# Zero-padding a 24-row product to 128 rows in a decoder-step kernel

## What is computed

```
S_new = exp(b_last)[..., None] * S + einsum('bshk,bshv->bhkv', kc, vc)   # s has one token
```

## Time and profile before

| what | value |
|---|---|
| timed runs, median | 1084.79 us |
| profiled execution, its own time | 1083.09 us |
| its span, first to last instruction | 1081.3 us |
| mean granted PE clock | 0.993 |
| PE busy | 1049.4 us (97%), 8530 matmuls |
| DVE busy | 570.6 us (53%) |
| ACT busy | 430.4 us (40%) |
| POOL busy | 1.4 us, 6 instructions |

### The profile page before, as it was taken

One profiled execution on the slowest core, in us unless ns is written; L12 is line 12 of the kernel. 1 busy time (PEld: TensorE's weight loads), 2 busy tenths in 40 slices (PEclk: granted clock), 3 DMA queues, 4 the chain that ended last, 5 costly groups with the idle time before them and its releaser, 6 DMA issues.

```text
span 1081.3 us, 21621 instructions
## 1 busy us (share of the span) xinstructions
PE 1049.4 (97%) x8530; PEld 1031.0 (95%) x8530; DVE 570.6 (53%) x1026; ACT 430.4 (40%) x586; POOL 1.4 (0%) x6
## 2 busy tenths in 40 slices
PE   6999999999999999999999997899999999999997
PEld 6999999999998899999999997799999999999997
DVE  5756655765665988633333333755545445422223
ACT  6443542444344888522222234732232332322222
POOL 0000000000000000000000000000000000000000
PEclk9999999999999999999999999999999999999999
DMA  7322232232222332333323343033233233133322
GB/s 216 98 81 78 80 99 73 85 99 80 80 88 67 89 87 83 94 87 97 94 82 95 97 158 98 20 98 90 85 97 96 78 97 92 55 92 96 95 78 79
DMA packets 182567, 98.23 MB, mean 91 GB/s; under 512 B 3784, under 2 KB 181192, under 8 KB 182408
## 3 DMA queue, kind: packets, MB, share of 16 engines
q1 hardware_dynamic: 164376, 88.62, 27.9%
q10 hardware_dynamic: 18080, 9.04, 2.8%
q0 software_dynamic: 80, 0.15, 0.0%
HBM read 90.79 MB, written 7.00 MB: 90 GB/s over the span
## 4 chain that ended last, share of the span: by engine, by line
PE 92%; DVE 3%; ACT 2%; DMA 1%; issue 1%; SPq 0%; DVEq 0%; ACTq 0%
PE proj L1178 79%; PE pr L1264 5%; DMA tmp<-in_x_prompt 1%; PE pi L1313 1%; PE pr L1318 1%; PE pr L1381 1%; PE pr L1287 1%; PE pi L1295 1%; PE pi L1381 1%; PE pi L1301 0%; ACT wh L320 0%; PE proj L1328 0%; DVE tmp L1077 0%; DVE acts L1065 0%; DVE raw L1157 0%
## 5 line engine op out<-in xcount | busy, mean ns | idle before, releaser
L1178 PE MATMUL proj<-acts,wh 128*128 128x260 f32 x4864 | 796.9, 286 | 11.1 <-DVE acts L1065 9.3
L1178 PEld LDWEIGHTS proj<-acts,wh 128*128 128x128 f32 x4864 | 668.7, 189 | 18.0 <-DVE acts L1065 10.9
L1178 PE MATMUL proj<-acts,wl 128*128 128x260 f32 x2432 | 490.7, 283 | 0.0
L1178 PEld LDWEIGHTS proj<-acts,wl 128*128 128x128 f32 x2432 | 375.5, 189 | 0.0
L681 DVE TENSOR_TENSOR wl<-raw,wh 128x1024 fp32r<-128x1024 f32 (+2 forms) x164 | 190.9, 1164 | 273.4 <-ACT wh L320 273.3
L320 ACT ACTIVATE wh<-raw 128x1024 fp32r<-128x1024 f32 (+2 forms) x164 | 165.8, 1011 | 355.7 <-PE proj L1178 352.5
L1264 PE MATMUL pr<-tmp 128*128 128x64 f32 (+1 forms) x512 | 65.8, 271 | 0.1
L1264 PEld LDWEIGHTS pr<-tmp 128*128 128x128 f32 x512 | 62.5, 191 | 0.9 <-DVE tmp L908 0.3
L766 DVE TENSOR_TENSOR tmp<-tmp 128x256 f32<-128x256 f32 x56 | 23.7, 423 | 24.4 <-PE pr L1264 24.3
L637 ACT ACTIVATE acts<-tmp 128x520 f32 (+1 forms) x21 | 13.5, 641 | 42.4 <-DVE tmp L1125 42.4
L634 ACT ACTIVATE tmp<-tmp 128x520 f32<-128x520 f32 x21 | 13.5, 641 | 40.0 <-DVE tmp L1116 40.0
(11 more groups left out here) (220 smaller groups left out, 747.3 us busy)
## 6 DMA issues: line engine op xcount, KB each, us to landing
raw<-in_w_in SPq DMA_DIRECT2D x64, 512.0 KB, 4.0
raw<-in_w_ffn_in SPq DMA_DIRECT2D x44, 512.0 KB, 3.7
raw<-in_w_ffn_out SPq DMA_DIRECT2D x16, 384.0 KB, 3.4
raw<-in_w_ffn_out SPq DMA_DIRECT2D x16, 320.0 KB, 3.2
tmp<-in_state_hgrn ACTq DMA_DIRECT2D x8, 512.0 KB, 4.1
out<-tmp ACTq DMA_DIRECT2D x8, 512.0 KB, 3.2
raw<-in_w_branch_a SPq DMA_DIRECT2D x8, 512.0 KB, 3.7
raw<-in_w_branch_b SPq DMA_DIRECT2D x8, 512.0 KB, 3.7
```

The source lines that it names most:

```text
L1178: o = mm(pp[par][:, hf, 0:TH], w, x[:, hf * TH:(hf + 1) * TH], start=start and n == 0, stop=stop and n == 2)
```

## The change

The product of `outer` runs over all 128 rows of `spare` instead of the first 24. For this the whole of `spare` is set to zero once, on POOL, at the start; the rows 24 to 127 stay zero afterwards. The first readers and writers of `spare` on ACT, DVE and PE get a wait for this, each head anew (always the same value, 1). Columns, weights' columns, count of matmuls and all else stay.

```diff
         @block.gpsimd
         def _(eng):
+            eng.memset(spare.bitcast(F32), 0.0).then_inc(E("pad_zero"), 1)
             eng.wait_ge(E("d_hl"), NH)
...
             def sample_rows(h):
+                eng.wait_ge(E("pad_zero"), 1)
                 eng.wait_ge(E("p_st"), h + 1)
                 act(STOK, PM[0:NS, 0:2 * P], AF.Copy).then_inc(E("a_st"), 1)
...
             def sample_values(h):
+                eng.wait_ge(E("pad_zero"), 1)
                 eng.wait_ge(E("a_st"), h + 1)
...
             def outer(h, k):
                 eng.wait_ge(E("d_vbd"), h + 1)
-                mm((PM, SB)[k], STOK[:, 0:P], VBD[:, k * 512:(k + 1) * 512], start=True, stop=True)\
+                if k == 0:
+                    eng.wait_ge(E("pad_zero"), 1)
+                mm((PM, SB)[k], spare[:, NB * P:(NB + 1) * P], spare[:, k * 512:(k + 1) * 512], start=True, stop=True)\
                     .then_inc(E("p_outer"), 1)
```

## The result

The changed kernel takes 1078.05 us (median of six runs, 1076.23 to 1079.53), against 1084.47 us for the kernel before (six runs, 1081.84 to 1086.07, among them the three given at the start). The ratio is 0.9949 with a 95% interval of 0.9936 to 0.9961, so 5.5 us faster (4.2 to 6.9). The two medians lie 6.4 us apart; the ratio, which comes with an interval, is the figure used here. Forecast were 5.25 us off and 1079.5 us. The profiled execution took 1078.69 us with a span of 1076.9.

The account below looks back on a forecast made before the run. PE was taken as the bound, busy for 97% of the span. Per head 0.80 less 0.05 us of wait, over seven heads 5.25 us, all else 0: 1084.79 - 5.25 = 1079.5 us, range 1077.0 to 1082.5.

Parts of the forecast that it names:

- The outer product's cost: At line 1307, one outer product costs 0.61 us, over 128 rows 0.22; gain used 0.40 each, 0.80 per head.
- The cause: At `outer`, PE empties and loads weights in the open, some 0.2 us either side, because only these products have under 128 rows.
- Waits for the state updates, heads 0 to 6: At line 1313, the 0.16 us slack goes and PE waits some 0.05 us per head, bounds 0 to 0.2.
- rival 4: State updates become the bound and the clock falls in every head: 6 us slower, 1090.7 us; chance 0.03.
- Head 7: State updates there don't wait for the outer products: gain 0, bounds 0 and 0.80; PE's 0.84 us wait becomes some 1.6.
- The low clock behind it: Behind head 7's wait the clock reads 0.54 for 3.4 us, losing about 1.6 us; no change taken, 1.6 either way.
- Zeroing and waits: One POOL memset of 2.8 us at the start and 24 waits, all hidden: cost 0, waits at most 0.4 us.
- No gain: At `outer`, the gap belongs to something else, or 24 rows cost what 128 cost: 1084.8 us; chance 0.05.
- half the gain: The 128-row product streams at line 1318's pace, 0.43 us instead of 0.22: 2.3 us off, 1082.5 us; chance 0.06.
- The third, more gain: Head 7 keeps its 0.8 us and the low clock behind it goes: 7.65 us off, 1077.1 us; chance 0.08.

Follow-up runs that it names:

- the exchange: At head 7, DVE's eight state updates moved ahead of its weight subtraction for the fourth unit: ratio 0.9917 on the changed kernel, 0.9971 on the kernel before.
- the pair with 24 rows: Kernel before, 24 rows, with the second outer product of each head moved up directly behind the first: ratio 0.9975, 2.7 us faster.

## Why the prediction was right

- *The outer product's cost.* 0.40 us per product was used; the chain shows 2 x 0.39 = 0.78 less a wait of 0.03, so some 0.75 per head, and seven heads gave 5.21 us where 5.25 stood. The 0.22 us for 128 rows, which no row showed, measured 0.23. Per head the saving was put 0.02 us too high and the wait 0.02 us too long; that the sum is met within 0.04 us is in part luck, and the timed 5.5 us (4.2 to 6.9) can't tell so finely.
- *The cause.* It was found by leaving out the 512 columns, the narrow output and the wait. The runs with 96 and 64 rows and with two products together show it by itself. What the prediction says, that only these products have fewer than 128 rows, holds from the heads on; ahead of them, lines 1229 and 1222 have eight products each of 12 and 124 rows, whose cost no row here shows. The rule of the Trainium skill that a change of the tiling mode drains the engine ("TensorEngine Tiling (Array Packing)", Key Properties) agrees with these runs, which show the price and not the drain itself; its list of modes ("Available Configurations") has 32 and 64 rows as such modes, and 24 and 64 measured alike (0.43 us in the chain). The list has modes of 32 columns too, but line 1273, with 24 columns of weights, showed no gap. The sentence that a product over 32 rows takes as long as one over 128 ("TensorE: Matmul & The Clock Gate", Why this matters for your kernels) holds for the second of two 24-row products (0.24 against 0.23 us), not for one among full products (0.61 us with what hangs on it).
- *Waits for the state updates, heads 0 to 6.* Forecast 0.05 us each, measured 0.03. The clock stayed at 1.00 in these heads, so rival 4 did not come. (The "0.2 x 7 = 1.05 more" of the range is the 0.15 above the forecast's 0.05, seven times.)
- *Head 7.* Gain 0 and a wait of 1.6 us forecast, 0 and 1.62 measured. The low clock behind it stayed, as forecast; but I had priced only the one stretch of it, and left out a second some 17 us later (last section), which by the run with 96 rows cost little.
- *Zeroing and waits.* Forecast 0; alone they gave 0.9998. The memset took 1.83 us where I had put 2.8, scaled from a short one on another engine, DVE.
- *The rivals.* No gain and half the gain fall with the chain above. The third, more gain, did not come: the low clock stayed. But the exchange shows that it was there to be had: 0.78 and 1.66 us for the 0.8 and 1.6 that I had priced, and with them the 0.84 us of the wait that the kernel before already had.

## What to carry to other kernels

Look for single products of few rows in a stream of full ones: where a matmul's next weights start only when it has ended, count start to start, not the busy time. Before padding, try to put such products next to each other, and pad the rows only as far as they give a gain (here 96 rows gave all of it, 64 nothing). And when PE is shortened, see at which waits it arrives earlier: the same 0.8 us were worth 0.75 in seven heads and nothing in the eighth, until its order on another engine was changed.

## What I had not expected

One wait of 0.84 us at head 7 cost some 2.5 us in the kernel before by the profiles, and 3.1 (2.0 to 4.3) by the timed runs. Behind it and the 16 one-column products the clock was at its lower level for some 3.4 us, and it fell again some 17 us later, behind a wait of 2.0 us for the second gate product. With the exchange the second drop is gone too, although a wait of 1.75 us for the gate product stays:

```profile
347.33 1.14 PE L1386 MATMUL pr<-tmp 128*128 128x260 f32 x4 [1.75 <-DVE tmp L939]
```

The clock reads 1.00 throughout there. But the length of this wait does not decide it: the kernel with 96 rows, without the exchange, waits 2.04 us at the same product, and its clock stays at 1.00 as well:

```profile
350.91 1.14 PE L1386 MATMUL pr<-tmp 128*128 128x260 f32 x4 [2.04 <-DVE tmp L939]
```
```profile
350.00:358.00 8.00, 5.92 (x41) 5.52 (x42) 7.77 (x15) 6.97 (x10) 0.00 (x0) 1.00 0.31 91
```

In the profiles the first drop stands in all seven kernels without the exchange and in none of the three with it; the second stands in six of the seven and in none of the three. What brings the second is open, and so is whether the exchange keeps it away.

The kernel before read 1081 to 1087 us over its runs, more than the 0.2% that I had taken for its scatter. The granted clock goes along with it: the shortest execution (1080.92 us) had a mean of 0.996, the longest (1087.12 us) one of 0.989. A single pair of runs could have missed a gain of 3 us, as that of the pair with 24 rows, and each ratio stands with its interval.
